# Second mixer of a two-block kernel: who builds P^T and C, quarter tiles in the last doubling level, and a reordered passage between the blocks

## The reference

```python
# end of the first block, start of the second
x = layer_norm(alpha * x + out, ln_g, ln_b)
hdn = rms_norm_2(x, norm_g) * (1.0 + scale) + shift
# gated DeltaNet, per head and chunk
decay = exp(where(lower, gc[:, None] - gc[None, :], -inf))
a_mat = where(strict, (kb @ k.T) * decay, 0.0)
t_mat = solve_triangular(a_mat + eye, eye)     # unit lower triangular inverse
u, w  = t_mat @ (v * beta), t_mat @ (kb * exp(gc))
qk    = where(lower, (q @ k.T) * decay, 0.0)
# over the chunks, in order
v_new = u - w @ state
o     = q_dec @ state + qk @ v_new
state = state * exp(g_last) + k_dec.T @ v_new
```

## Time and profile before

| What | Value |
|---|---|
| median of 3 runs | 1125.43 us (1124.95 to 1127.58) |
| the profiled execution: its time, its span | 1124.68 us, 1122.9 us |
| TensorE busy, share of the span | 1070.3 us, 95% |
| VectorE, ScalarE, GpSimd busy | 680.2, 446.3, 235.3 us |
| mean granted clock of TensorE | 0.986 |

### The profile page before, as it was taken

How to read it: one execution, slowest core, us unless ns; L and a number is a source line. 1 busy time by engine, 2 the same in 40 slices (tenths; PEclk the granted TensorE clock), 3 DMA queues, 4 the chain that set the end, 5 groups by cost and what they waited for, 6 DMA issues and landing times. The chain is left out here.

```text
span 1122.9 us, 14447 instructions
## 1 busy us (share of the span) xinstructions
PE 1070.3 (95%) x5558; PEld 889.2 (79%) x5558; DVE 680.2 (61%) x1132; ACT 446.3 (40%) x821; POOL 235.3 (21%) x167
## 2 busy tenths in 40 slices
PE   7999999999899999999799999999999986999997
PEld 4888888888688877788678788888878975889886
DVE  4245426632166678546836756667875669976635
ACT  4223214333256553141423333367525456325432
POOL 0001000000000143001100100004204756245792
PEclk9999999999999899989999999999999999999999
DMA  8276534332121222032333445343212211203501
GB/s 295 86 265 230 186 113 133 111 96 72 61 100 48 98 97 75 1 132 76 129 107 113 150 150 188 113 164 117 94 57 94 92 61 57 75 19 100 183 1 75
DMA packets 58305, 123.95 MB, mean 110 GB/s; under 512 B 5760, under 2 KB 5888, under 8 KB 58112
## 3 DMA queue, kind: packets, MB, share of 16 engines
q1 hardware_dynamic: 55792, 110.22, 29.0%
q0 software_dynamic: 2304, 12.58, 3.2%
q10 hardware_dynamic: 144, 0.26, 0.1%
HBM read 108.90 MB, written 14.16 MB: 110 GB/s over the span
## 5 line engine op out<-in xcount | busy, mean ns | idle before, releaser
L287 DVE TENSOR_TENSOR w_lo<-raw,w_hi 128x2048 fp32r<-128x2048 f32 x58 | 135.1, 2329 | 213.8 <-ACT w_hi L283 207.1
L283 ACT ACTIVATE w_hi<-raw 128x2048 fp32r<-128x2048 f32 x51 | 97.6, 1913 | 222.4 <-PE projections_ps L131 138.3
L129 PE MATMUL projections_ps<-projections_x_hi,w_hi 128*128 128x512 f32 x208 | 81.1, 390 | 0.4 <-ACTq L503 0.4
L130 PE MATMUL projections_ps<-projections_x_lo,w_hi 128*128 128x512 f32 x208 | 80.9, 389 | 0.0
L131 PE MATMUL projections_ps<-projections_x_hi,w_lo 128*128 128x512 f32 x208 | 80.9, 389 | 0.0
L129 PE MATMUL projections_ps<-w_hi,projections_x_hi 128*128 128x512 f32 x192 | 74.7, 389 | 0.0
L130 PE MATMUL projections_ps<-w_lo,projections_x_hi 128*128 128x512 f32 x192 | 74.7, 389 | 0.0
L131 PE MATMUL projections_ps<-w_hi,projections_x_lo 128*128 128x512 f32 x192 | 74.7, 389 | 0.0
L244 DVE SCALAR_TENSOR_TENSOR resid<-resid,mixer_cw 128x512 f32<-128x512 f32 x96 | 64.9, 746 | 0.0
L2405 POOL TENSOR_TENSOR mixer_es<-masks,mixer_gsel 128x1024 f32<-128x1024 f32 x8 | 18.3, 2293 | 213.1 <-PE mixer_ps L1875 134.1
L129 PE MATMUL output_ps<-w_hi,output_m_hi 128*128 128x512 f32 x128 | 54.1, 423 | 1.1 <-DVE output_m_lo L1246 0.7
(11 more groups left out here) (319 smaller groups left out, 2641.8 us busy)
## 6 DMA issues: line engine op xcount, KB each, us to landing
raw<-in_w_in SPq DMA_DIRECT2D x26, 1024.0 KB, 5.0
raw<-in_gdn_w_in SPq DMA_DIRECT2D x24, 1024.0 KB, 5.1
tok<-in_ada_w POOLq DMA_DIRECT2D x16, 768.0 KB, 6.2
raw<-in_w_out SPq DMA_DIRECT2D x8, 1024.0 KB, 5.0
qkv_kept<-mixer_ring SPq DMA_DIRECT2D x8, 1024.0 KB, 4.2
mixer_st<-qkv_kept SPq DMA_DIRECT2D x32, 256.0 KB, 2.9
raw<-in_gdn_w_out SPq DMA_DIRECT2D x8, 1024.0 KB, 5.6
resid<-in_att_bias SPq DMA_DIRECT2D x16, 256.0 KB, 2.8
```

Source lines behind the costliest of these rows:

```text
L129: nc.tensor.matmul(out, w_hi, x_hi, start=first, stop=False, skip_group_check=True)
L130: nc.tensor.matmul(out, w_hi, x_lo, start=False, stop=False, skip_group_check=True)
L283: self.nc.scalar.activation(self.hi[s][:], self.raw[s][:], ACT.Copy).then_inc(self.hi_ready, 1)
L287: engine.tensor_tensor(self.lo[s][:], self.raw[s][:], self.hi[s][:], ALU.subtract)\
```

## The change

Five edits. (1) In the first block's tail, `before_factor(t + 1)` is written ahead of `after_factor(t)`, GpSimd's `layer_factor(t + 1)` ahead of `last_factor(t)`, and the multiplication into `tok` of tiles 0 to 2 goes from VectorE to ScalarE, behind the next tile's square. (2) TensorE's transposes 4 to 7 of the second block are interleaved with the first output tile of the projection. (3) VectorE no longer masks K K; `C` is scaled straight from the bank in two operations, and `kk_out`'s second count comes behind them. (4) `PT` is made by VectorE behind `C`, no longer by GpSimd. (5) In the second doubling level V, Z and the transposes of `U` work on the one 64x64 quarter that is used, ScalarE copies that quarter, and VectorE's merge under a mask becomes a plain copy of it.

```diff
@@ scalar, first block
+                if t:
+                    act.wait_ge(factor_ok, ROW_FACTOR[t - 1])
+                    nc.scalar.activation(tok[:, t - 1, 0:D_MODEL], resid[:, t - 1, :], ACT.Copy, scale=row_f[:, t - 1:t])
@@ gpsimd, first block
+            layer_factor(0)
             for t in range(TT):
-                layer_factor(t)
+                if t + 1 < TT:
+                    layer_factor(t + 1)
                 last_factor(t)
@@ vector, first block
+            step = before_factor(0)
             for t in range(TT):
-                step = before_factor(t)
-                if t:
-
-                    dve.wait_ge(factor_ok, 2 * t + 2)
-                    nc.vector.tensor_scalar(tok[:, t - 1, 0:D_MODEL], resid[:, t - 1, :], row_f[:, t - 1:t], None, ALU.mult)
+                next_step = before_factor(t + 1) if t + 1 < TT else None
                 after_factor(t, step)
+                step = next_step
@@ tensor, second block
                         if e == 0:
+                            if s == 0:
+                                turn_x(4 + kk)
                             pe.wait_ge(low_ok, k + 1)
@@ double(i, j, kind, lv, grp)
-                    if kind == "V":
+                    if lv and kind == "V":
+
+                        mm = nc.tensor.matmul(out[LOW, 0:64], C[UP, 8 * j + m, 64:P], T[UP, m, 0:64], start=True, stop=True)
+                    elif lv:
+                        mm = nc.tensor.matmul(out[UP, 64:P], V[LOW, m, 0:64], U[j % 2][LOW, m, 64:P], start=True, stop=True)
+                    elif kind == "V":
                         mm = nc.tensor.matmul(out, C[:, 8 * j + m, :], T[:, m, :], start=True, stop=True)
...
-                        mm = nc.tensor.transpose(out, U[j % 2][:, m, :], ident)
+                        mm = nc.tensor.transpose(out[UP, 0:64], U[j % 2][UP, m, 0:64], ident[UP, 0:64])
@@ evacuate(i, j, kind, lv, grp)
+                    if lv:
+                        nc.scalar.activation(V[LOW, ms4, 0:64], src[LOW, :, 0:64], ACT.Copy).then_inc(v_out, 1)
...
-                    nc.scalar.activation(T[:, ms4, :], src, ACT.Copy).then_inc(t_out, 1)
+                    nc.scalar.activation(T[UP, ms4, 0:64], src[UP, :, 0:64], ACT.Copy).then_inc(t_out, 1)
@@ gpsimd, second block
-                    pool.wait_ge(e_ok, at(i, 1, j, 1))
-                    pool.wait_ge(kk_out, at(i, 2, j, 2))
...
-                    nc.gpsimd.tensor_tensor(PT[:, 8 * j:8 * j + 8, :].rearrange("p (h c) e -> p h c e", h=2),
-                                            E.rearrange("p (h c) e -> p h c e", h=2),
-                                            KQm.unsqueeze(1).broadcast_to([P, 2, TT, P]), ALU.mult).then_inc(pt_ok, 1)
@@ scale_kq(i, j)
-                nc.vector.tensor_tensor(KKm, four[:, 0], strict.unsqueeze(1).broadcast_to([P, TT, P]), ALU.mult)\
-                    .then_inc(kk_out, 1)
...
+                for h in range(2):
+                    scaled = nc.vector.tensor_tensor(C_j[:, h], four[:, 0], nbp[:, j, h].unsqueeze(2).broadcast_to([P, TT, P]),
+                                                     ALU.mult)
+                scaled.then_inc(kk_out, 1)
+                dve.wait_ge(e_ok, at(i, 1, j, 1))
                 dve.wait_ge(kk_out, at(i, 2, j, 2))
...
+                E_j = E.rearrange("p (h c) e -> p h c e", h=2)
+                nc.vector.tensor_tensor(C_j, C_j, E_j, ALU.mult).then_inc(c_ok, 1)
...
+                nc.vector.tensor_tensor(PT[:, 8 * j:8 * j + 8, :].rearrange("p (h c) e -> p h c e", h=2), E_j,
+                                        KQm.unsqueeze(1).broadcast_to(shape), ALU.mult).then_inc(pt_ok, 1)
@@ doubled(i, j, kind, lv, grp)
+                    if lv:
+                        nc.vector.tensor_copy(U[j % 2][UP, 4 * grp:4 * grp + 4, 64:P],
+                                              psZ[UP, grp, :].rearrange("p (m c) -> p m c", c=P)[:, :, 64:P]).then_inc(u_ok2, 1)
+                        return
```

More of the change, by code:

```diff
@@ L66, in block_masks @@
     j, l = np.arange(P)[:, None], np.arange(P)[None, :]
-    levels = [(j // (2 * b) == l // (2 * b)) & (j // b < l // b) for b in (32, 64)]
+    levels = [(j // (2 * b) == l // (2 * b)) & (j // b < l // b) for b in (32,)]
     return np.stack([j < l, j // 32 == l // 32] + levels, 1).astype(np.float32)
@@ L926, in scan_and_output @@
         mod_sum = sem("mod_sum")
+        LAYER_FACTOR, ROW_FACTOR = (3, 4, 6, 8), (5, 7, 9, 10)
         block = ctx.enter_context(nc.Block())
@@ L1387, in after_factor @@
             def after_factor(t, step):
-                dve.wait_ge(factor_ok, 2 * t + 3)
+                dve.wait_ge(factor_ok, LAYER_FACTOR[t])
                 own.wait(step)
@@ L1429, in second_mixer @@
         es = sb("es", [P, 2, 8, P])
-        masks2 = sb("masks2", [P, 4, P])
+        masks2 = sb("masks2", [P, 3, P])
         decays = sb("decays", [P, 3, TT, V_HEADS])
@@ L1489, in second_mixer @@
         U = [space_u[:, s] for s in range(2)]
-        KKm = space_u[:, 0, 0:4]
         KQm = space_u[:, 0, 4:8]
@@ L1621, in doubling_parts @@
             return parts
+        UP, LOW = slice(0, 64), slice(64, P)
         SLOTS = (1, 3, 4, 5, 7, 8, 9, 11, 12, 13)
@@ L1759, in _, with turn_x @@
             pe.sem_inc(banks_free, 1)
-            pe.wait_ge(xn_ok, 1)
-            for e in range(KT):
+            def turn_x(e):
                 if e >= 4:
@@ L1768, in _ @@
                 tr.then_inc(h_turned, 1)
+            pe.wait_ge(xn_ok, 1)
+            for e in range(4):
+                turn_x(e)
             pe.wait_ge(banks_free, 1)
@@ L2234, in evacuate @@
                         act.wait_ge(z_made, at(i, 4, j - 1, 2 + q))
-                    nc.scalar.activation(V[:, ms4, :], src, ACT.Copy).then_inc(v_out, 1)
+                    if lv:
+                        nc.scalar.activation(V[LOW, ms4, 0:64], src[LOW, :, 0:64], ACT.Copy).then_inc(v_out, 1)
+                    else:
+                        nc.scalar.activation(V[:, ms4, :], src, ACT.Copy).then_inc(v_out, 1)
                 elif kind == "T":
                     act.wait_ge(t_made, at(i, 2, j, q))
-                    nc.scalar.activation(T[:, ms4, :], src, ACT.Copy).then_inc(t_out, 1)
+                    nc.scalar.activation(T[UP, ms4, 0:64], src[UP, :, 0:64], ACT.Copy).then_inc(t_out, 1)
             def out_squares(i, j, c):
@@ L2463, in _ @@
                         log_decay_steps(i, j + 1)
-                    pool.wait_ge(e_ok, at(i, 1, j, 1))
-                    pool.wait_ge(kk_out, at(i, 2, j, 2))
-                    if i == 0 and j == 0:
-                        for b in range(2):
-                            pool.wait_ge(spilled[b], 16 * (B_CONV // 2))
-                    nc.gpsimd.tensor_tensor(PT[:, 8 * j:8 * j + 8, :].rearrange("p (h c) e -> p h c e", h=2),
-                                            E.rearrange("p (h c) e -> p h c e", h=2),
-                                            KQm.unsqueeze(1).broadcast_to([P, 2, TT, P]), ALU.mult).then_inc(pt_ok, 1)
                 pool.wait_ge(kss_ok, at(i, 1, HB - 1, 1))
@@ L2599, in scale_kq @@
                     .then_inc(kk_out, 1)
-                dve.wait_ge(kk_out, at(i, 2, j, 2))
-                own.wait()
-                C_j, shape = C[:, 8 * j:8 * j + 8, :].rearrange("p (h c) e -> p h c e", h=2), [P, 2, TT, P]
-                own.did(nc.vector.tensor_tensor(C_j, KKm.unsqueeze(1).broadcast_to(shape),
-                                                nbp[:, j].unsqueeze(3).broadcast_to(shape), ALU.mult))
-                dve.wait_ge(e_ok, at(i, 1, j, 1))
-                own.wait()
-                nc.vector.tensor_tensor(C_j, C_j, E.rearrange("p (h c) e -> p h c e", h=2), ALU.mult).then_inc(c_ok, 1)
+                C_j, shape = C[:, 8 * j:8 * j + 8, :].rearrange("p (h c) e -> p h c e", h=2), [P, 2, TT, P]
+                own.wait()
+                for h in range(2):
[3 more added lines that the diff above has]
+                dve.wait_ge(e_ok, at(i, 1, j, 1))
+                dve.wait_ge(kk_out, at(i, 2, j, 2))
+                E_j = E.rearrange("p (h c) e -> p h c e", h=2)
+                nc.vector.tensor_tensor(C_j, C_j, E_j, ALU.mult).then_inc(c_ok, 1)
+                if i == 0 and j == 0:
+                    for b in range(2):
+                        dve.wait_ge(spilled[b], 16 * (B_CONV // 2))
+                nc.vector.tensor_tensor(PT[:, 8 * j:8 * j + 8, :].rearrange("p (h c) e -> p h c e", h=2), E_j,
+                                        KQm.unsqueeze(1).broadcast_to(shape), ALU.mult).then_inc(pt_ok, 1)
             def factors(i):
@@ L2652, in doubled @@
                     dve.wait_ge(z_made, at(i, 4, j, 2 * lv + grp + 1))
-                    level = masks2[:, 2 + lv, :].bitcast(mybir.dt.int32)
+                    if lv:
+                        nc.vector.tensor_copy(U[j % 2][UP, 4 * grp:4 * grp + 4, 64:P],
+                                              psZ[UP, grp, :].rearrange("p (m c) -> p m c", c=P)[:, :, 64:P]).then_inc(u_ok2, 1)
```

(2 more changed lines are left out.)

## The result

In the first measurement the changed kernel takes 1111.9 us (median of 4 runs, 1110.4 to 1113.1), the kernel before 1126.5 (4 runs, 1125.0 to 1127.6): a ratio of 0.988, interval 0.986 to 0.991. That is 14.6 us less, where 20 were predicted.

A forecast was written before the change was run, and what follows sets the result against it. TensorE was taken to set the pace nearly everywhere. Passage 2.4, builds 5.5, loops 8 and pair 0 3.8 sum to 19.7 us, from 1124.68 to 1105.0 (median 1105.5); range 1100 to 1110, or 1112 with B and part of A.

The forecast's parts named there:

- The loops: Chunk loops: quarter tiles save 1.5 us in four loops and 1.0 in two, 8 us in all (1.6 to 10.8).
- Rival D: Chunk loops: each switch of rows costs 0.2 us more, builds bring 1 us, so no change, 1125 us; chance 0.03.
- my 15.7 us: Chunk loops: turn_v would come every 15.7 us in place of 17.3.
- Rival C: Chunk loops: thinner quarter products drop the clock to 1.2 GHz, up to 15 us more a loop, kernel slower; chance 0.04.
- The sum: Whole kernel: 2.4 + 5.5 + 8 + 3.8 = 19.7 us off the profiled 1124.68, giving 1105.0, as median 1105.5.
- The builds: Builds of half 1: without GpSimd's product VectorE needs 5.0 us a build, not 7.95; gain 5.5 us, at least 1.
- Rival B: Builds: GpSimd's steps meet the product for C, so builds bring 1 us; 15.2 us in all, 1110; chance 0.10.
- The passage: Between the blocks: reordered tail and interleaved transposes bring 2.4 us (1.5 to 3.8).
- the interleaving: Second block's start: first projection tile ends at 553.0 rather than 555.0, 2.0 us gained.
- the tail: First block's end: ScalarE's four operations end at 543.7 against 544.20, 0.4 us gained (0 to 1.8).
- Pair 0: Its doubling, standing alone in each half: 6.2 us becomes 4.3, 1.9 us twice, 3.8 (2 if TensorE gains nothing).
- Rival A: Doubling: quarter tiles no cheaper than full ones, loops 1.6, pair 0 2; 11.5 us in all, 1114; chance 0.11.

The follow-up runs named there:

- e9: The changed kernel with the last level's V and Z products over all 128 rows and the transposes whole again: 1109.0 us (0.9854).
- the two later medians: The changed kernel measured again, unaltered, in two later series: 1106.7 us (0.9831) and 1107.4 us (0.9825).
- e1: The kernel before with edit 5 alone: 1117.7 us (0.9923).
- e3: The kernel before with edits 1 and 2 alone: 1123.6 us (0.9972).
- e8: The changed kernel with 128 identity products of several tile shapes behind the first turn_v of half 1; quarter tiles took 0.056 us an instruction.

## Why the prediction was right and wrong

**The loops (the step that failed).** "I take 0.06: 0.48 us a group against 0.89" was right for the group by itself (8 instructions of 0.056). What failed is the sentence behind it, "a change of rows seems to cost 0.06 to 0.1 us". It is no change of rows but of the stationary tile's size, it costs 0.16 to 0.19 in the products by themselves, and it is paid twice a group, part of it by the neighbour. In the loop that is 0.60 a group and 0.1 to 0.2 at each full neighbour. Rival D had named the mechanism, at 0.2 us a change above my 0.06 to 0.1; the runs put it at about 0.1 above. TensorE's own work falls by 0.5 us a loop, the wait at `turn_v` by 0.4: 0.9 and not 1.5, and 0.4 and not 1.0 in the third loop of a half, 4.4 us and not 8. L1792's row had 32 rows and 32 moving columns at once; I read the one dimension and missed that a small group's start tells only one of its two changes. That the transposes in chunk 2 bring nothing came true, and by VectorE's chain as I had said (e9, above). Whether the loop would have reached my 15.7 us if changes cost nothing, no run shows.

**The clock.** Rival C had the right engine and the wrong place and size. No loop loses its clock by its own quarter groups, as forecast; but its sign, a clock under 1.00 in a loop, stands in the first loop of a half, where a dip runs on from the doubling of pair 0 or begins right behind it. There the edit thins TensorE's work between waits that stay, and the dip costs 1.3 to 1.6 us (2.8 once) in some halves, not up to 15. (At 15 us a loop, three loops would have given up to 1150 us; the 1130 of rival C does not follow from its own terms.) In the first profile that is 2.9 us. I had worked out the doubling's own gain, 1.9 us, and it came (2.0), without asking what the emptier stretch does to the next one.

**The profiled execution as base.** The sum stood on an execution of 1124.68, whose untouched code up to the passage took 534.4 us. In other executions the same code takes 531.2 to 537.6. A range of the forecast must hold that as well; mine did in part, and 1111.9 lies at its edge. (By its own terms the sum gives 1105.0 + 0.75, so 1105.7 and not 1105.5.) That the two later medians, 20.2 and 19.7 us less than before, lie so near the forecast is luck in part: the loops bring 3.6 us less than it says, and the builds, the passage and the clock of those executions make it up.

**The builds.** 5.5 predicted, 5.6 in the first profile, 6.9 where no dip falls into them (25.59 us, thirteen profiles), 27.0 us where one does (three). Before's own builds hold a dip (32.5 us), those of e1 one as well (31.5) and those of e3 two (31.9). So dip against dip the edits bring 4.6 to 5.6 us, and the further 1.4 is the clock, which falls in three of sixteen profiles of the new builds and in all three of the old. Rival B's collision is there, once in four: the product for C, L2620, takes 1.97 us beside GpSimd's `steps`, and 1.23 elsewhere:
```profile
932.56 1.90 POOL L2426 TENSOR_TENSOR mixer_es<-masks,mixer_gsel 128x1024 f32<-128x1024 f32 x1 [5.73 <-PE mixer_ps L1888]
...
933.57 1.97 DVE L2620 TENSOR_TENSOR resid<-resid,mixer_es 128x1024 f32<-128x1024 f32 x1 [0.17 <-ACT mixer_es L2234]
...
939.21 1.23 DVE L2620 TENSOR_TENSOR resid<-resid,mixer_es 128x1024 f32<-128x1024 f32 x1 [0.24 <-ACT mixer_es L2234]
```
It costs VectorE 0.7 us; what it costs the stage no run shows.

**The passage.** 2.4 predicted, 2.8 measured: the interleaving 1.7 for 2.0, the tail 1.1 for 0.4. Of ScalarE's four operations I counted the last `tok` as well, but the last root needs only the square before it: the square, at 543.39, is read before the last `tok` begins, and the root ends at 545.43, 8.6 us behind L1108 where it was 9.8.
```profile
543.39 1.04 ACT L1182 ACTIVATE output_junk<-resid 128x1024 f32<-128x1024 f32 x1
...
544.42 1.13 ACT L1187 ACTIVATE tok<-resid,row_f 128x1024 f32<-128x1024 f32 x1
...
544.88 0.55 POOL L1201 TENSOR_TENSOR row_f<-row_f,output_half_neg 128x1 f32<-128x1 f32 x1
```
**Pair 0.** 3.8 predicted, 4.0 measured. **Rival A** (no cheaper tiles) falls with e8. The Trainium skill's rule that a load overlaps only where row groups differ ("TensorE: Matmul & The Clock Gate", Part 3, The mechanism) stands half: e8 has 0.056 us an instruction in the same rows against 0.036 in turn between two row groups, so same-row quarters are not the 0.9 us a group that it would give, but different row groups do overlap more.

## What to carry to other kernels

Before a product is cut to a quarter, count how often the stationary tile's size changes: here each change took back about 0.17 us, what one and a half products had saved, so small tiles pay in long rows of their own and hardly as single groups among full ones. Where an edit thins an engine's work between waits that stay, look at the granted clock behind it; and compare stages from the same instruction in several executions, since the untouched code here moved by 6.4 us, more than twice what the passage gained.

## What the runs showed of the hardware

- A change in the size of the stationary tile costs TensorE 0.16 us (columns) to 0.19 us (rows), whole tiles against halves; the moving length none (0.45 us for a pair whose parts take 0.22 and 0.23).
- f32 instructions with 64x64 tiles follow each other by 0.056 us in the same rows and by 0.036 in turn between upper and lower rows; with 128 rows and 64 columns by 0.063; with 128 stationary columns and 64 moving, or half the rows, by 0.116 and 0.118.
- The granted clock fell to 0.50 for about 3.4 us behind stretches in which TensorE was busy 1.5 to 1.7 of 2 us, in some executions and not in others (seven of nine in half 1, one of eight in half 0), and in none of the three where the same waits were filled with products of no use.
- A VectorE product of two 128x1024 operands took 1.23 us, 1.97 beside a GpSimd product of 1.90 us, and before the change 3.19 beside one of 3.33 us.
